# State stage of a hybrid decoder layer: head mask and rotation table prepared in attention, zeros of the tap table read from DRAM, the state chain in two halves

## The reference, cut to what matters

```
ug = u.reshape(b, l, 32 groups, 16)                       # u: 512 columns of the projection
bu = einsum('blgc,gpc->blgp', ug, B_discrete)             # 64 complex states for each group
s_t = A_discrete * s_{t-1} + bu_t                         # complex recurrence over 1024 tokens (or one, from s0, for a sample)
y = einsum('blgp,gcp->blgc', s_re, c_re) - einsum('blgp,gcp->blgc', s_im, c_im) + d_skip * u
g = gelu(y);  out = g * sigmoid(g @ w_glu + b_glu)
outputs: y, and the last state of the prompt and of each sample
```

## Time and profile before

| | |
|---|---|
| three runs | 2840.46, 2843.67, 2855.08 us (median 2843.67) |
| the profiled execution | 2848.97 us, of which the span of the trace is 2847.3 us |
| PE (matmul) busy | 2616.9 us, 92% of the span |
| DVE busy | 2042.4 us, 72% |
| ACT busy | 848.9 us, 30% |
| POOL busy | 374.4 us, 13% |
| mean granted TensorE clock | 0.963 of full |
| read from and written to HBM | 452.96 MB and 22.36 MB |

### The profile page before, as it was taken

How to read it: one execution, slowest core, us unless ns; L and a number is a source line. 1 busy time by engine, 2 the same in 40 slices (tenths; PEclk the granted TensorE clock), 3 DMA queues, 4 the chain that set the end, 5 groups by cost and what they waited for, 6 DMA issues and landing times. The chain is left out here.

```text
span 2847.3 us, 46030 instructions
## 1 busy us (share of the span) xinstructions
PE 2616.9 (92%) x15819; PEld 2117.8 (74%) x15819; DVE 2042.4 (72%) x2814; ACT 848.9 (30%) x1538; POOL 374.4 (13%) x588
## 2 busy tenths in 40 slices
PE   6779899999999999998859889998989999999998
PEld 4457666666666667875534689884979999999998
DVE  6549999988998956777773273538367677777767
ACT  4231112111122124018941451413233222222225
POOL 1010032322223220220042000033000000000000
PEclk8789999999999999999989989999989999999999
DMA  9876699989899863544167641126101112111121
GB/s 354 299 259 201 177 326 327 333 301 324 298 332 341 314 203 130 151 123 96 32 192 252 237 134 52 45 82 229 53 23 46 59 44 59 44 44 44 44 59 75
DMA packets 346757, 479.78 MB, mean 169 GB/s; under 512 B 35400, under 2 KB 228293, under 8 KB 344750
## 3 DMA queue, kind: packets, MB, share of 16 engines
q1 hardware_dynamic: 303718, 334.87, 35.9%
q0 software_dynamic: 42448, 142.33, 14.4%
q10 hardware_dynamic: 408, 0.31, 0.0%
HBM read 452.96 MB, written 22.36 MB: 167 GB/s over the span
## 5 line engine op out<-in xcount | busy, mean ns | idle before, releaser
L111 PE MATMUL banks<-ffn_ghi,whi 128*128 128x344 f32 (+1 forms) x880 | 318.0, 361 | 18.8 <-DVE xT L2249 10.4
L84 ACT ACTIVATE whi<-raw 128x1024 fp32r<-128x1024 f32 (+1 forms) x118 | 121.4, 1041 | 675.1 <-PE banks L113 582.8
L113 PE MATMUL banks<-ffn_ghi,wlo 128*128 128x344 f32 (+1 forms) x880 | 310.1, 352 | 0.0
L112 PE MATMUL banks<-ffn_glo,whi 128*128 128x344 f32 (+1 forms) x880 | 308.8, 351 | 0.0
L111 PE MATMUL banks<-a_hhi,whi 128*128 128x512 f32 x704 | 287.9, 409 | 6.9 <-DVE wlo L88 6.1
L611 POOL DMA_DIRECT2D ffn_vt<-in_cache_v_dram x384 | 206.1, 537 | 656.0 <-issue 651.0
L624 DVE TENSOR_TENSOR ffn_kt<-ffn_kt,ffn_q 128x1024 f32<-128x1024 f32 x224 | 272.4, 1216 | 24.2 <-DMA ffn_kt<-in_cache_k_dram 24.0
L113 PE MATMUL banks<-a_hhi,wlo 128*128 128x512 f32 x704 | 278.4, 395 | 0.0
L112 PE MATMUL banks<-a_hlo,whi 128*128 128x512 f32 x704 | 278.2, 395 | 0.0
L629 DVE TENSOR_REDUCE ffn_z<-ffn_kt 128x16 f32<-128x1024 f32 x224 | 272.5, 1217 | 5.7
L111 PEld LDWEIGHTS banks<-ffn_ghi,whi 128*128 128x128 f32 x880 | 166.4, 189 | 67.4 <-issue 23.5
(11 more groups left out here) (506 smaller groups left out, 5938.0 us busy)
## 6 DMA issues: line engine op xcount, KB each, us to landing
ffn_kt<-in_cache_k_dram SPq DMA_DIRECT2D x448, 256.0 KB, 4.4
ffn_vt<-in_cache_v_dram POOLq DMA_DIRECT2D x384, 256.0 KB, 5.0
raw<-in_w_ffn_gate_dram SPq DMA_DIRECT2D x44, 512.0 KB, 5.1
raw<-in_w_ffn_up_dram SPq DMA_DIRECT2D x44, 512.0 KB, 5.1
raw<-in_w_ffn_down_dram SPq DMA_DIRECT2D x44, 512.0 KB, 4.6
last_kt<-in_cache_k_dram POOLq DMA_DIRECT2D x64, 256.0 KB, 3.1
s_vt<-in_cache_v_dram POOLq DMA_DIRECT2D x64, 256.0 KB, 5.5
s_vt<-in_cache_v_dram SPq DMA_DIRECT2D x64, 256.0 KB, 7.3
```

Of the source, the lines that this page charges most:

```text
L84: act.activation(self.k.whi[c % W_RING][:, 0:self.width], self.slots[s][:, 0:self.width], ACT.Copy).then_inc(self.hi_done, 1)
L111: pe.matmul(out, whi, rhi, start=first, stop=False)
L112: pe.matmul(out, whi, rlo, start=False, stop=False)
L113: return pe.matmul(out, wlo, rhi, start=False, stop=last)
```

## The change

1. samples_ahead stores the taps in a DRAM table with twice the columns: for each of 16 rows and 32 groups, 128 columns for zeros and then the 128 taps. The store is now one of 512 pieces of 512 bytes.
2. Attention: POOL clears a small tile, and SP stores it as the zeros of that table (256 KB). After the third pair's outputs SP loads rot (2 MB) into its place of the state stage. After the last v_rows, POOL makes the head mask.
3. State stage, SP and POOL: rot's loads, the clearing of toep and the mask are gone. Each toep copy now brings the zeros along: 16 partitions x 32 x 512 bytes, 256 KB, where copy l had (8 - l) x 32 KB.
4. State stage, DVE: the chain's 18 steps of 128 x 2048 become two halves of 18 steps of 128 x 1024; the first half starts after 8 gsum quads.
5. State stage, PE: weigh(8) in place of weigh(13), a wait for the first half of the chain and for toep, y quads 0 to 3 with two quads of values behind each, one quad of values, a wait for the whole chain, "final", y quads 4 to 7 and the ysample quads with one each.
6. first_half: its squares' ring goes from 6 to 3 tiles, two of three squares and all roots go behind later y quads, and PE's column sums behind the eighth y quad. w_glu is loaded once 29 of 32 quads of values are weighed, without a wait for the turns.

```diff
-        self.kg_dram = scratch("kg_scratch", [16, 32 * P])
+        self.kg_dram = scratch("kg_scratch", [16, 32 * 2 * P])
...
-                pool.dma_start(self.kg_dram, kg[:, :, :].rearrange("p g n -> p (g n)")).then_inc(q["stored_kernels"], 16)
+                pool.dma_start(self.kg_dram.rearrange("c (g n) -> c g n", g=G)[:, :, P:2 * P], kg[:, :, :]).then_inc(q["stored_kernels"], 16)
...
+                sp.wait_ge(S["zeros"], 1)
+                sp.dma_start(self.kg_dram.rearrange("c (g a n) -> (c g) a n", g=8, a=4)[:, :, 0:P], zeros[:, :, :]).then_inc(self.zeros_kept, 16)
...
+                    if j == 2:
+                        sp.wait_ge(S["z_ps"], first_chunk[2 * BLOCKS])
+                        for i in range(2):
+                            sp.dma_start(self.ssm_rot_sb[i][:, :, :].rearrange("p t n -> p (t n)"), self.rot_dram[i]).then_inc(self.rot_in, 16)
...
+                pool.memset(zeros[:, :, :], 0.0).then_inc(S["zeros"], 1)
+                pool.wait_ge(S["v_rows"], 2 * PAIRS)
+                Values.make_mask(pool, self.late_mask, self.mask_made)
...
-                for i in range(2):
-                    sp.dma_start(rot[i][:, :, :].rearrange("p t n -> p (t n)"), self.rot_dram[i]).then_inc(q["rot_in"], 16)
...
-                sp.wait_ge(q["cleared"], 1)
+                sp.wait_ge(self.zeros_kept, 16)
...
-                    sp.dma_start(toep[l * C:(l + 1) * C, :, l * C:P], taps[:, :, 0:(L - l) * C]).then_inc(q["toep_in"], 16)
+                    sp.dma_start(toep[l * C:(l + 1) * C, :, :], taps[:, :, P - l * C:2 * P - l * C]).then_inc(q["toep_in"], 16)
...
-                sp.wait_ge(late_v.v_used, 16 * Values.COUNT)
-                glu.sp(sp)
...
+                sp.wait_ge(late_v.v_used, 16 * Values.COUNT - 3)
+                glu.sp(sp)
...
                 late_v.prepare(pool)
-                pool.memset(toep[:, :, :], 0.0).then_inc(q["cleared"], 1)
-                late_v.make_mask(pool)
                 late_v.load(pool, 0, late_v.OTHERS)
...
+                for half in range(2):
+                    th = slice(half * H, half * H + H)
+                    R0, R1 = rot[0][:, th, :], rot[1][:, th, :]
+                    g0, g1 = S[0][:, th, 1:SW], S[1][:, th, 1:SW]
+                    v.wait_ge(q["taken"], kinds["gsum"] + (half + 1) * H)
...
-                weigh(13)
-                pe.wait_ge(q["v"], self.ssm_states)
-                b = quad("final", 0)
...
+                weigh(8)
+                pe.wait_ge(q["v"], self.ssm_early)
                 pe.wait_ge(q["toep_in"], 16 * L)
                 pe.wait_ge(q["ck_in"], 32)
                 for kind in ("y", "ysample"):
                     for i in range(8):
+                        if kind == "y" and i == EARLY:
+                            weigh(1)
+                            pe.wait_ge(q["v"], self.ssm_states)
+                            b = quad("final", 0)
...
-                        if kind == "y" and i == 1:
+                        if kind == "y" and i == 7:
                             for t_ in range(3):
                                 self.first_half.sums(pe, t_)
-                        weigh(1)
+                        weigh(2 if kind == "y" and i < EARLY else 1)
```

More of the change, by code:

```diff
@@ L2487, in attention @@
         self.ssm_smalls = nc.alloc_sbuf_tensor_at("s_smalls", [P, 560], F32, offset=self.x_offset + 30 * 1024 + 64)
+        self.ssm_rot_sb = [self.place(f"s_rot{i}", [P, 16, P], at) for i, at in enumerate((16, 32.125))]
+        self.late_mask = self.place("s_vmask", [P, 512], 45.5)
+        zeros = self.place("at_zeros", [P, 4, P], 28, ring=True)
         hide = self.place("at_hide", [P, P], 25, ring=True)
@@ L2724, in ssm @@
         place = self.place
-        rot = [place(f"s_rot{i}", [P, T, P], 8 * i) for i in range(2)]
+        rot = self.ssm_rot_sb
         ck = [place(f"s_ck{i}", [P, T, L + 1, C], 81 + 9 * i) for i in range(2)]
         gm = self.ssm_gm
-        toep = place("s_toep", [P, G, P], 115)
+        toep = place("s_toep", [P, G, P], 115.25)
         smalls = self.ssm_smalls
@@ L2761, in ssm, with number @@
         quads, kinds = 0, {}
-        for kind, n in (("gsum", 16), ("final", 1), ("y", 8), ("ysample", 8), ("turn", 9)):
+        EARLY = 4
+        for kind, n in (("gsum", 16), ("y_early", EARLY), ("final", 1), ("y_late", 8 - EARLY), ("ysample", 8), ("turn", 9)):
             kinds[kind] = quads
             quads += n
+        def number(kind, i):
+            if kind == "y":
+                return kinds["y_early"] + i if i < EARLY else kinds["y_late"] + i - EARLY
+            return kinds[kind] + i
         with nc.Block() as block:
@@ L2806, in take @@
                 def take(kind, i, out, in_, func=ACT.Copy, last=True, **kw):
-                    act.wait_ge(q["quad"], kinds[kind] + i + 1)
+                    act.wait_ge(q["quad"], number(kind, i) + 1)
                     ins = act.activation(out, in_, func, **kw)
@@ L2812, in bank, with take_y @@
                 def bank(kind, i):
-                    return ps[(kinds[kind] + i) % 4]
+                    return ps[number(kind, i) % 4]
+                def take_y(i):
+                    take("y", i, yg[:, :, :].rearrange("p l (g c) -> p g l c", c=C)[:, groups_of(i)],
+                         bank("y", i).rearrange("p (g l c) -> p g l c", g=4, l=L), ACT.Gelu_apprx_tanh)
                 for i in range(16):
@@ L2819, in _ @@
                 late_v.last_weights(act)
-                for t_ in range(2):
-                    self.first_half.squares(act, t_)
+                self.first_half.squares(act, 0)
+                for i in range(EARLY):
+                    take_y(i)
                 take("final", 0, srows[0:T, 0:2].rearrange("p i x -> p (i x)"), bank("final", 0)[0:T, 0:2 * P], last=False)
                 take("final", 0, srows[:, 2:4].rearrange("p i x -> p (i x)"), bank("final", 0)[:, 2 * P:4 * P])
[L2824 to L2830, removed]
+                for t_ in range(1, 3):
+                    self.first_half.squares(act, t_)
+                for i in range(EARLY, 8):
+                    take_y(i)
+                for t_ in range(3):
+                    self.first_half.roots(act, t_)
                 for i in range(8):
@@ L2835, in _ @@
                     if i == 6:
+                        act.wait_ge(late_v.v_used, 16 * Values.COUNT)
                         for n in range(2):
@@ L2880, in cmul @@
                         tt(im, t0, t1, ALU.add)
[L2881 to L2884, removed]
+                H = T // 2
+                v3 = lambda x: x[:, :].rearrange("p (t j) -> p t j", t=H)
+                v.wait_ge(self.rot_in, 32)
                 v.wait_ge(self.smalls_in, 16)
-                v.wait_ge(q["taken"], kinds["gsum"] + 16)
@@ L2888, in _ @@
[L2888 to L2898, removed]
@@ L2978, in _ @@
                     for i in range(8):
+                        if kind == "y" and i == EARLY:
+                            weigh(1)
+                            pe.wait_ge(q["v"], self.ssm_states)
+                            b = quad("final", 0)
+                            for j in range(2):
+                                turn(b[0:T, j * P:(j + 1) * P], sn[:, 2 + j, 0], self.ident[:, :])
+                            for j in range(2):
+                                ins = turn(b[:, (2 + j) * P:(3 + j) * P], sn[:, j].rearrange("p b t -> p (b t)"), self.ident[:, :])
+                            done(ins)
                         b = quad(kind, i)
```

75 lines of the change are left out of this document (41 added, 34 removed).

## The result

The changed kernel takes 2856.23 us (median of 18 runs, 2840.04 to 2861.92), the kernel before 2843.71 us (median of 18 in the same comparison, 2837.20 to 2855.08). The ratio is 1.0033, 95% interval 1.0020 to 1.0046, that is 5.7 to 13.1 us slower. It lies within 0.5%, the bound named in the prediction for no change, but beyond its own interval and above the predicted range of 2829 to 2853. The profiled execution took 2856.6 us, its span is 2854.9 us, 7.6 us over that of before.

A forecast was written before the change was run, and what follows sets the result against it. PE, 92% busy, bounds most of the kernel; in the state stage DMA time ahead of y does. The stage's -2.4 us and +1 us for the kg store gave -1.4 us: 2842 us, range 2829 to 2853.

The forecast's parts named there:

- a ledger of DMA time ahead of y: State stage: pages, ck and toep copies through busy DMA engines set y's start, 1507.9, 10.1 us earlier than before.
- The first half of the chain: State stage, DVE: about 20 us of work, done at about 1477, covered because pages and toep come later.
- The mask in attention: Attention: making the mask there costs nothing, as DVE has 7 us free; without that slack up to 2.3 us.
- The store of kg: samples_ahead: a later landing of this store delays ACT's copies; taken at +1 us, bounds nothing to +5.1 us.
- The quads and "final": State stage: five quads of values now inside y give back 5.3 us, "final" 0.4 us.
- the clock: State stage, PE: idle before y, it runs y's first 3 to 4 us at half speed, costing 2 us.
- a toep copy at 2.2 us: State stage: each of eight 256 KB copies takes 2.2 us of DMA time, 17.6 us together; bounds 0.66 and 4.3 us.
- rival B: State stage: dearer toep copies, no gain from 2.4 us each, up to +15.4 us; sign y after 1515; chance 0.15 above +5 us.
- The return to 2.4 GHz: State stage, PE: in the earlier profile work began at 1492.11 and full clock returned at about 1494.9.
- The sum of the stage: State stage: -10.1 + 5.3 + 0.4 + 2 = -2.4 us.
- A: State stage: cheap toep copies thanks to 512-byte pieces, 0.66 us each, total -13.7 us; chance 0.2 for a gain above 9 us.
- C: State stage: POOL's gap in issuing pages was the bound; y starts at 1480, total -30 us, 2813; chance 0.04.

The follow-up runs named there:

- e7: The kernel before the change with only the head mask made in attention; 2846.95 us, ratio 1.0003 to the kernel before.
- e2: The changed kernel with POOL clearing toep again and the eight copies bringing only the taps, 256 to 32 KB; 2841.30 us, ratio 0.9985 to before.
- e4: The changed kernel plus 13 unused products between the eighth quad and y, to keep PE busy; 2849.91 us, ratio 1.0029 to before.
- e1: The changed kernel with toep's table laid out in DRAM in attention and each of eight loads going into all 128 partitions; 2839.43 us, ratio 0.9987 to before.
- e9: The changed kernel with its own eight toep copies all issued right behind ck, ahead of SP's other pages; 2835.59 us, ratio 0.9951 to before.
- e5: The changed kernel with toep's table loaded over all 128 partitions, the eight loads right behind ck; 2826.70 us, ratio 0.9937 to before.
- e8: As e5, but with the table's rows contiguous in DRAM, so pieces of 2 KB; 2825.00 us, ratio 0.9930 to before.
- e10: As e8, but with 5 quads of values weighed ahead of y in place of 8; 2828.42 us, ratio 0.9920 to before.

## Why the prediction was wrong

**What held.** The view was right: a ledger of DMA time ahead of y, not POOL's gap (e7), and not the chain. The first half of the chain ended 26.4 us after gsum (1483.6), 25.8 was forecast; the whole chain 50.5, 49.8 forecast. Neither was waited for. y began behind a wait for toep, as forecast. The mask in attention is free:

```profile
1409.36 0.52 POOL L892 MEMSET s_vmask<- 128x512 f32 x1 [118.85 <-ACT at_v_rows L2607]
...
1416.23 0.68 POOL L899 TENSOR_SCALAR_AFFINE_SELECT s_vmask<-s_vmask 32x512 f32<-32x512 f32 x1
```

Attention takes 167.7 us up to gsum, 167.1 before. The store of kg was set at +1 us and cost nothing. The lines of after for the earlier trace rows:

```profile
136.03 1.15 ACT L1245 ACTIVATE a_hhi<-a_scaled 128x512 fp32r<-128x512 f32 x2 [16.39 <-DMA kg_scratch<-a_kg]
```

```profile
kg_scratch<-a_kg POOLq DMA_DIRECT2D x1, 256.0 KB, 6.4
```

The quads and "final" moved behind the start of y were set at 5.7 us; 10.5 us less the clock's 5.2 leaves 5.3.

**The step that failed: a toep copy at 2.2 us.** The prediction's ledger with after's numbers: data flow from 1458.5, 16.4 us for 16 pages and ck, 32 pages at 386 GB/s are 21.7, the last landing 1: 1497.6. y started at 1520.8, so 23.2 us remain for eight copies, 2.9 us each. The mechanism was the one of the forecast and of rival B, the size was not. The prediction had put 2.5 us to a copy alone and lowered it, with the ground that a stretch with both queues was cheaper. That ground does not hold: with both queues at work the windows of after move 225, 237 and 209 GB/s, less than the 296 of that stretch. The copies in it were 32 to 96 KB, and e2 shows that their price goes by bytes. 0.7 us a copy, eight times, is 5.6 us of y's start.

The 2.5 us had a weak source as well. The window 1474:1476 of before does not hold copy 0 alone:

```profile
DMA packets 71, 0.21 MB, mean 104 GB/s; under 512 B 15, under 2 KB 15, under 8 KB 62
```

Copy 0 went in pieces of 16 KB, but 47 of the 71 lie between 2 and 8 KB and only 9 are larger. By the sizes in the trace the 47 are a page's pieces, 5 are ck's and 4 are of copy 0. So its 104 GB/s are those of a mix, and no row shows one copy alone; what the runs show is the 102 GB/s of e2.

**The smaller errors.** 48 pages stood ahead, not 46: 1.3 us. Together this is 6.9 us, the whole of what y started late against the forecast (63.6 after gsum, 56.7 forecast). The clock was set at 2 us and took 5.2 (e4). The gap ahead of y was right (17 us forecast, 1491 to 1508; 16.82 measured), though it lies later, as the eighth quad was weighed at 1504. The return to 2.4 GHz was not: the one row of before had PE back at full clock 3 us after it took up work, and in after it took over 11 us. The sum of the stage: -2.4 forecast, + 5.6 + 1.3 + 3.2 - 0.4 = +7.3, the measured value. The copy's price is found from the start of y itself, so this agreement tests no term by itself. The kg store gives back 1 us of the total.

**The rivals.** B (dearer copies, and from 2.4 us no gain) is what happened. Its sign, a start of y after 1515, is met by the trace (1520.8), but 6.0 us of that lie ahead of gsum, and without them it is 1514.8. A had the right remedy in a wrong place: the copies can be as cheap as it said, but by the partitions they write and not by their pieces. Made so, in e1, the table's transfers are 2.0 us cheaper each. C fell with e7.

The Trainium skill ("SBUF — State Buffer", section "Door 1: The DMA port swizzle") states that partitions 0 to 15 reach 4 of SBUF's 16 DMA ports and gives 104 GB/s for them, measured with 1 MiB. The runs agree, with 102 GB/s from e2. By that page's figure a copy is an estimated 2.5 us (262 KB at 104 GB/s). The 512-byte rule, which the prediction weighed in its place (the Trainium skill, "DMA: Bandwidth & Descriptors", Specifications), did not decide: e1 and after have the same pieces and differ by 16 us.

At e2's 102 GB/s a copy of 262 KB is 2.6 us, and after's took 2.9. The ledger of e2 leaves 14.2 us for its 1.18 MB, of which 11.6 are bytes at 102 GB/s: again 0.3 us a copy, though they are smaller. What these 0.3 us are is open; in e9, without pages between them, a copy took 1.9 us.

**What is open.** The medians differ by 12.5 us and the stage by 7.3, from one profile each. The interval of the ratio (5.7 to 13.1 us) holds both, and no stage but this one differs beyond what identical code shows between executions. Where the other 5 us are is not shown.

## What to carry to other kernels

Price a DMA by the partitions that it writes as well as by its bytes: the same 256 KB in the same pieces cost 2.0 us more into 16 partitions than into 128, so a shifted or replicated table is best laid out in DRAM at a quiet time and loaded over all partitions. A change that lets work start earlier is worth what the last of its inputs allows; here a start on half a chain was worth 14 us or nothing, depending on where eight loads stood in a queue. And when a wait is shortened by thinning the work ahead of it, look at the granted clock behind the wait.

## What the runs showed that had not been expected

- Copies into different groups of 16 partitions seem to overlap in part when issued back to back (138 GB/s, e2's 102): they cost 1.0 us more than spread loads (e9 against e5), and 2.0 us more when pages stand between them (after against e1).
- Spread over 128 partitions, a 256 KB load in 512-byte pieces cost y's start 0.5 us more than one in 2 KB pieces (e5 against e8, 3.8 us for eight, one profile each), and it held SP's queue three times as long.
- PE's clock stayed at 0.50 for the first 11 us of dense work in after and for 12 us in e10, and it was 1.00 from the first products of y in e4, where PE had been kept busy.
